# Hybrid-mixer trunk on one core: norm factors applied behind the matmuls instead of in front of them

## What is computed

```
h    = x * rsqrt(mean(x*x) + eps) * norm1_g      # per token factor, per channel weight
proj = h @ w_in                                   # 48 blocks of 128 channels, and dt (16 channels)
gate = sigmoid(h @ w_gate)                        # four branches
x    = x + merged(proj, gate, branches) @ w_out
h2   = x * rsqrt(mean(x*x) + eps) * norm2_g
x    = x + (silu(h2 @ wg) * (h2 @ wu)) @ wd       # layer 0: dense mixer; layer 1: top-2-of-8 experts
```

## Time and profile before

| | us |
|---|---|
| median of 3 runs | 1944.27 |
| lowest, highest | 1943.65, 1946.18 |
| profiled execution, device time | 1946.46 |
| its span, first to last instruction | 1944.6 |
| TensorE busy | 1888.2 (97%) |
| VectorE, ScalarE, GpSimd busy | 1477.2, 1173.1, 313.3 |
| mean granted TensorE clock | 0.993 of full speed |

### The profile page before, as it was taken

How to read it: one execution, slowest core, us unless ns; L and a number is a source line. 1 busy time by engine, 2 the same in 40 slices (tenths; PEclk the granted TensorE clock), 3 DMA queues, 4 the chain that set the end, 5 groups by cost and what they waited for, 6 DMA issues and landing times.

```text
span 1944.6 us, 27985 instructions
## 1 busy us (share of the span) xinstructions
PE 1888.2 (97%) x10637; PEld 1640.5 (84%) x10637; DVE 1477.2 (76%) x1312; ACT 1173.1 (60%) x939; POOL 313.3 (16%) x256
## 2 busy tenths in 40 slices
PE   6999999999999999999999999999999999999997
PEld 6999878899989998778788888888888878888785
DVE  5775667745565775676788988898889888898887
ACT  4555454333335445544677777677776776777775
POOL 1047660000000156920510000000000000000000
PEclk9999999999999999999999999999999999999999
DMA  5444444345543444446599999999999999999994
GB/s 223 174 152 152 173 165 173 138 179 188 178 165 131 174 172 162 146 170 251 199 363 367 359 370 351 361 364 371 360 360 353 381 346 358 374 360 370 355 358 161
DMA packets 71490, 510.80 MB, mean 263 GB/s; under 512 B 7936, under 2 KB 8192, under 8 KB 10368
## 3 DMA queue, kind: packets, MB, share of 16 engines
q1 hardware_dynamic: 70128, 505.15, 69.0%
q0 software_dynamic: 1296, 4.72, 0.6%
HBM read 507.74 MB, written 2.10 MB: 262 GB/s over the span
## 4 chain that ended last, share of the span: by engine, by line
PE 73%; DVE 10%; ACT 6%; POOL 6%; issue 4%; DMA 0%; DVEq 0%; SPq 0%; ACTq 0%; POOLq 0%
PE psum L1270 71%; DVE weight_lo L679 3%; POOL proj_r L1219 3%; POOL proj_r L1220 3%; ACT weight_hi L376 2%; DVE weight_lo L646 2%; DVE scr L792 2%; ACT weight_hi L395 2%; PE psum L1680 1%; ACT y_hi L527 1%; DVE scr L787 1%; ACT proj L447 1%; DVE proj L1013 0%; DMA weight_raw<-mix_w 0%; DVE proj L670 0%
## 5 line engine op out<-in xcount | busy, mean ns | idle before, releaser
L1270 PE MATMUL psum<-weight_hi,y_hi 128*128 128x512 f32 x1440 | 572.3, 397 | 14.1 <-DVE weight_lo L679 11.2
L1270 PE MATMUL psum<-weight_hi,y_lo 128*128 128x512 f32 x1440 | 563.3, 391 | 0.0
L1270 PE MATMUL psum<-weight_lo,y_hi 128*128 128x512 f32 x1440 | 562.5, 391 | 0.0
L646 DVE TENSOR_TENSOR weight_lo<-weight_raw,weight_hi 128x2048 fp32r<-128x2048 f32 x141 | 324.5, 2303 | 236.6 <-ACT weight_hi L376 235.8
L679 DVE TENSOR_TENSOR weight_lo<-weight_raw,weight_hi 128x2048 fp32r<-128x2048 f32 x165 | 377.7, 2289 | 95.7 <-ACT weight_hi L395 95.6
L395 ACT ACTIVATE weight_hi<-proj 128x2048 fp32r<-128x2048 f32 x169 | 324.2, 1925 | 127.5 <-PE psum L1270 127.5
L679 DVE TENSOR_TENSOR weight_lo<-proj,weight_hi 128x2048 fp32r<-128x2048 f32 x169 | 385.6, 2289 | 12.1 <-ACT weight_hi L395 10.6
L1270 PE MATMUL psum<-h_hi,weight_hi 128*128 128x256 f32 x1248 | 359.6, 288 | 9.1 <-DVE h_lo L649 6.4
L1270 PE MATMUL psum<-h_lo,weight_hi 128*128 128x256 f32 x1248 | 356.1, 285 | 0.0
L1270 PE MATMUL psum<-h_hi,weight_lo 128*128 128x256 f32 x1248 | 356.0, 285 | 0.0
L376 ACT ACTIVATE weight_hi<-weight_raw 128x2048 fp32r<-128x2048 f32 x141 | 268.7, 1908 | 142.9 <-PE psum L1270 140.8
(11 more groups left out here) (280 smaller groups left out, 1881.2 us busy)
## 6 DMA issues: line engine op xcount, KB each, us to landing
proj<-moe_w SPq DMA_DIRECT2D x169, 1024.0 KB, 6.2
weight_raw<-moe_w SPq DMA_DIRECT2D x165, 1024.0 KB, 5.9
weight_raw<-mix_w SPq DMA_DIRECT2D x108, 1024.0 KB, 4.8
weight_raw<-ff_w SPq DMA_DIRECT2D x33, 1024.0 KB, 4.7
first_raw<-moe_w SPq DMA_DIRECT2D x2, 1024.0 KB, 5.8
par<-par_in SPq DMA_DIRECT2D x2, 768.0 KB, 9.6
x<-x_in SPq DMA_DIRECT2D x2, 512.0 KB, 4.5
token_rows<-x POOLq DMA_DIRECT2D x2, 512.0 KB, 3.2
```

The lines of the kernel that those rows point to most:

```text
L646: V.tensor_tensor(lo[:, slot, :], raw[:, slot, :], hi[:, slot, :].bitcast(f32), ALU.subtract).then_inc(lo_done, 1)
L1270: return nc.tensor.matmul(o, a, b_, start=start, stop=stop, skip_group_check=True, **k)
```

## The change

The matmuls of the mixers and of the dense mixer run on x times the norm weight, split in high and low, without the factor per token. The factor is applied to the results: VectorE multiplies each bank of the projection by a row of factors (`rstd_row`) as it takes it out of PSUM, where ScalarE copied it before; the gates' sigmoids take it as the scale operand (there tokens lie on the partitions), dt likewise; in the dense mixer VectorE scales both banks, with silu behind the first. The sums and the spread of the factors move on TensorE from in front of unit 0 to the stage dt_row, which stands now behind unit 1, and in the dense mixer to the end and the middle of its first two units. Squares move from VectorE to ScalarE. Convolution 0 moves to behind unit 2. In the dense mixer and into layer 1, x's high and low parts are made behind each output bank. At the start SyncE loads par first, then halves of x and halves of unit 0 by turns, and con behind unit 1. The idle matmuls at the norms go.

```diff
 PLAN = (
-    ("lead", 1), ("dt_row", 1), ("conv0", 1), ("dt_in", 1), ...
+    ("lead", 2), ("dt_row", 1), ("conv0", 0), ("dt_in", 1), ...
 SyncE
-            for half in range(2):
-                sp.dma_start(x[:, 4 * half:4 * half + 4, :], ...)
-            sp.dma_start(con[:], con_in).then_inc(con_loaded, 16)
+            sp.dma_start(par[:, :PAR_FIRST], par_in[0, :, :PAR_FIRST]).then_inc(par_loaded, 16)
+            for part in range(2):
+                sp.dma_start(x[:, 4 * part:4 * part + 4, :], ...)
+                some = slice(part * UNIT // 2, (part + 1) * UNIT // 2)
+                sp.dma_start(raw[:, 0, some], mix_w[0, 0, :, some]).then_inc((first_landed, raw_landed[0])[part], 16)
             for layer in range(DEPTH):
...
-                for j in range(RING):
+                for j in range(0 if layer else 1, RING):
                     load(mix_w[layer, j, :, :], base_of(layer), j)
+                    if layer == 0 and j == 1:
+                        sp.dma_start(con[:], con_in).then_inc(con_loaded, 16)
 ScalarE
+            def high(n, q):
...
+                if n:
+                    act.wait_ge(S["x_sum"], PAIRS * (n - 1) + q + 1)
+                for k in (2 * q, 2 * q + 1):
+                    last = A(to[:, k, :], x[:, k, :], ACT.Copy, scale=gain[:, k:k + 1])
+                last.then_inc(S["h_hi_done"], 1)
+            def squares(q):
+                A(flat(sq[:, 2 * q:2 * q + 2, :]), flat(x[:, 2 * q:2 * q + 2, :]), ACT.Square).then_inc(S["sq_done"], 1)
+            def norm_row(n):
+                act.wait_ge(S["rstd_ps"], n + 1)
+                A(rstd_row[:], bank(7)[:, 0:SEQ], ACT.Copy).then_inc(S["rstd_row"], 1)
             mixer_unit:
                 if u < IN_UNITS:
-                    used(b + u)
-                    A(flat(proj[:, 2 * u:2 * u + 2, :]), bank(u % 4), ACT.Copy).then_inc(S["win_done"], 1)
+                    pass
...
-                        A(gate_of(step)[:, 0, :], bank(0), ACT.Sigmoid).then_inc(S["gate_done"], 1)
+                        A(gate_of(step)[:, 0, :], bank(0), ACT.Sigmoid, scale=rstd[:, 0, :]).then_inc(S["gate_done"], 1)
...
+                elif u >= U_OUT and layer == 0:
+                    high(1, u - U_OUT)
+                    squares(u - U_OUT)
             stage:
                 if kind == "dt_row":
+                    norm_std(2 * layer)
                     act.wait_ge(S["dt_sum"], layer + 1)
                     A(row[:], bank(6)[0:HEADS, 0:SEQ], ACT.Copy).then_inc(S["dt_row"], 1)
+                    norm_row(2 * layer)
             before the units of a layer:
+                if layer == 0:
+                    for part in range(2):
+                        act.wait_ge(x_loaded[part], 16)
+                        high(0, 2 * part)
+                        high(0, 2 * part + 1)
+                        first_half(part)
+                    split(0, 1)
+                    for q in range(PAIRS):
+                        squares(q)
+                else:
+                    for q in range(PAIRS):
+                        high(2 * layer, q)
+                        squares(q)
             dense mixer:
-                        act.wait_ge(unit_used, RING + f0 + 2 + RING * i + 1)
-                        act.wait_ge(S["mult_done"], i + 1)
-                        A(ff_g, bank(4), ACT.Silu).then_inc(S["silu_done"], 1)
+                        act.wait_ge(S["g_scaled"], i + 2)
+                        A(ff_g, ff_g, ACT.Silu).then_inc(S["silu_done"], 1)
 VectorE
+            def low(n, q):
...
+                dve.wait_ge(S["h_hi_done"], PAIRS * n + q + 1)
+                for k in (2 * q, 2 * q + 1):
+                    last = V.scalar_tensor_tensor(to[:, k, :], x[:, k, :], gain[:, k:k + 1], from_hi[:, k, :].bitcast(f32), ALU.mult, ALU.subtract)
+                last.then_inc(S["h_lo_done"], 1)
+            def scaled(out_, b):
+                return V.tensor_tensor(tiles(out_), tiles(bank(b)), rstd_pair, ALU.mult)
+            def evacuated(layer, u):
+                dve.wait_ge(unit_used, RING + base_of(layer) + u + 1)
+                scaled(flat(proj[:, 2 * u:2 * u + 2, :]), u % 4).then_inc(S["win_done"], 1)
             mixer_unit, behind split(b, u + AHEAD):
+                if 2 <= u < IN_UNITS:
+                    evacuated(layer, u)
...
                         dve.wait_ge(unit_used, RING + b + u + 1)
                         added(q)
+                        if q:
+                            low(1, q - 1)
+                        if q == PAIRS - 1:
+                            low(1, q)
             stage:
+                if kind == "dt_row":
+                    norm_diag(2 * layer)
+                    dve.wait_ge(S["rstd_row"], 2 * layer + 1)
+                    evacuated(layer, 0)
+                    evacuated(layer, 1)
                 elif kind == "dt_in":
-                        last = V.tensor_tensor(small[:, 1, t, :], raw_dt[:, t, :], P_("dt_bias"), ALU.add)
+                        last = V.scalar_tensor_tensor(small[:, 1, t, :], raw_dt[:, t, :], rstd[:, t, :], P_("dt_bias"), ALU.mult, ALU.add)
             dense mixer, hidden(i):
-                        V.tensor_tensor(ff_h, ff_g, bank(5), ALU.mult).then_inc(S["mult_done"], 1)
+                        scaled(ff_h, 5).then_inc(S["u_scaled"], 1)
+                        dve.wait_ge(S["u_scaled"], i + 1)
+                        dve.wait_ge(S["silu_done"], i + 1)
+                        V.tensor_tensor(ff_h, ff_g, ff_h, ALU.mult).then_inc(S["mult_done"], 1)
 TensorE
             tile_pair: an argument early; t = 0 and 1 with k < early first, then both with the rest
...
             mixer_unit, u == 0:
+                    elif layer:
+                        tile_pair(0, b, 0, (S["h_lo_done"], 2 * PAIRS * layer), 6)
+                    else:
+                        pe.wait_ge(S["first_lo"], 1)
+                        tile_pair(0, b, 0, (S["h_lo_done"], 0), between=lambda: split_is(0))
             stage:
                 if kind == "dt_row":
+                    pe.wait_ge(con_loaded, 16)
+                    pe.wait_ge(S["masks_done"], 1)
+                    norm_sums(2 * layer)
                     pe.wait_ge(S["wdt_lo"], layer + 1)
...
                     last.then_inc(S["dt_sum"], 1)
+                    norm_spread(2 * layer)
             dense mixer:
-                    tile_pair(4, f0, 0, (S["h_lo_done"], PAIRS))
+                    tile_pair(4, f0, 0, (S["h_lo_done"], PAIRS), 6, a)
+                    norm_sums(1)
                     split_is(f0 + 1)
-                    tile_pair(5, f0, 1)
+                    tile_pair(5, f0, 1, a=a, between=lambda: norm_spread(1))
...
-                        pe.wait_ge(S["silu_done"], i + 1)
+                        pe.wait_ge(S["g_scaled"], i + 1)
```

More of the change, by code:

```diff
@@ L1292, in tile_pair @@
                         last = product(bank(b_out)[:, t * SEQ:(t + 1) * SEQ], (first + j) % RING, KT * t + k,
-                                       h_hi[:, k, :], h_lo[:, k, :], k == 0, k == KT - 1)
+                                       a[0][:, k, :], a[1][:, k, :], k == 0 and (early == KT or t == 0), k == KT - 1)
+                    if n == 0 and between:
+                        between()
                 last.then_inc(unit_used, 1)
```

166 lines of the change are left out of this document (82 added, 84 removed).

## The result

The changed kernel takes **1952.55 us**, the median of 5 runs (1952.28 to 1955.07); the kernel before, timed beside it, 1946.18 (1943.65 to 1946.18, 5 runs). The ratio is 1.0042, with a 95% interval from 1.0029 to 1.0054: slower, by about 0.4%. In the experiments the kernel before was timed 7 to 15 times in each session, and its medians were 1943.4 to 1944.3; against these the difference of the medians is some 8.4 instead of 6.4 (the ratio, made from all runs, says 8.2). The kernel after was timed in the first session alone, five times; where later runs are set against its 1952.55, a difference carries 2 to 3 us of doubt. The profiled execution took 1952.28 us with a span of 1950.5, against 1946.46 and 1944.6 before: +5.9. Forecast were +9.4 and 1953.7.

A forecast was written before the change was run, and what follows sets the result against it. A loop of VectorE and ScalarE, as long as TensorE's work, was taken to become the projection's bound. Start -8.2, dense boundary -2.3, layer 1 -7.6, loop +22.2, clock +5.1, gates +0.2: +9.4 onto 1944.27, 1953.7 us; range 1936 to 1961.

The forecast's parts named there:

- the five places named: Projection: TensorE waits before units 6, 8, the transposes, unit 16 and the spread, released by VectorE; +11.1 us per layer.
- 15 us a layer: Sign that the forecast is right: TensorE's idle time at five places of each projection, released by VectorE.
- The clock, +5.1: TensorE falls to half clock behind new projection waits: three falls more than before, +5.1 us, bounds 0 and 6.8.
- The start, -8.2: Kernel start: first weight matmul at 9.2, unit 2 at 27.2 instead of 35.4, so 8.2 us saved.
- The bound of -4: Kernel start, if halves of weights land later: only 4 of the 8.2 us stay, total 1957.7.
- Into the dense mixer, -2.3: Boundary behind mixer layer 0: a 6.05 us chain per unit, a 4.0 wait, 2.3 us saved; bounds -7.6 and 0.
- The last `down`: End of the dense mixer: one scaling more in front of a wait of 2.06, 0.7 us later.
- Into layer 1: Boundary behind the dense mixer: a wait of 0.8, unit 2 at 590.1 instead of 597.7, so 7.6 us saved.
- the case with GpSimd first: Convolution 6: GpSimd's addition starts before VectorE's pair and holds it up, 1.2 us longer per layer, total 1960.
- Faster: Rival: evacuations hide in VectorE's idle time, boundaries alone count, -18.1 us, total 1926.2; chance 0.18.
- half hidden: Projection: variant of the faster rival, evacuations half hidden, without falls of the clock, total 1937.3.
- Even: Rival: projection loop as worked out, no clock falls in it or the dense boundary, +2.6 us, 1946.9; chance 0.17.

The follow-up runs named there:

- e1: Changed kernel, with ScalarE issuing the split of the next weights ahead of the silu in units of convolutions 1 to 7: 1924.14 us, ratio 0.9898.
- e10: Changed kernel, with VectorE's evacuation of unit u-1 ahead of the low part of unit u+2, in place of unit u's behind it: 1934.56 us, ratio 0.9947.
- e3: Kernel before, with VectorE instead of ScalarE copying the banks of all 24 projection units, as plain copies: 1962.97 us, ratio 1.0100.
- e4: Changed kernel, with ScalarE copying the banks of units 2 to 23 as before, without their token factors: 1934.09 us, ratio 0.9955.
- e11: Kernel before, with idle matmuls in TensorE's waits of over 1.2 us and behind the norm's spread at both boundaries: 1940.88 us, ratio 0.9984.
- e9: Changed kernel, with idle matmuls of ones_r ahead of all long waits of TensorE: 1946.22 us, ratio 1.0016.
- e5: Changed kernel, with ScalarE's high part and squares behind the split of the next output unit in layer 0: 1947.36 us, ratio 1.0011.
- e7: Changed kernel, with 17 idle matmuls in the 4.3 us wait of the first dense unit alone: 1954.5 us.

## Why the prediction was right, and where it was not

**The sign and the mechanism held.** The waits stand at the five places named, and VectorE ends them, before the transposes by way of ScalarE's silu. Forecast were 1.8, 2.2, 2.6, 4.0 and 4.0; the rows have 1.48, 1.92, 0.79 (layer 1: 2.27), 3.93 and 1.98 (layer 1: 0.90). The 0.1 before unit 14 did not show. The sign "15 us a layer" did not come true as it stands: the five waits make 10.1 and 10.5, since a fall of the clock ahead of a wait eats into it. Behind one fall of 1.7 the spread waits 1.98, which makes the 3.7 of the forecast's 4.0. e1 and e10 tell that it is the loop and its order, e3 that the evacuations make 9.4 of the stage's 10.3, e4 that some 1 us per layer is the changed start of the stage. Without falls the stage is 10.3 longer, against 11.2 forecast with the first gate unit: 1.8 too much over both layers.

**The number was in part luck.** The forecast median was 1953.7, the measured one 1952.55. But the forecast difference was +9.4, and +5.9 came between the profiled executions. The boundaries erred by 3.3 one way, loop and clock by 6.9 the other, and the base of the forecast, 1944.27, lay 1.9 below the median of the kernel before that was timed beside the changed one.

**The clock, +5.1, was the worst step.** It counted three more falls in the stages, at full price: four that nothing hides, behind the transposes and the spread of each layer, less the one of before. In the profiled executions it is one (behind the transposes of layer 1) against one (143.9 in layer 0 of before, 142.4 in e11), and net they cost nothing: 8.7 and 11.9 of the table add up to 20.6, which is twice the 10.3 of the runs without falls. What was wrong: falls came also behind the waits of 1.92 and 3.93, where the text had them hidden, and there they were hidden indeed; but by doing so they shortened the next waits, of the transposes (0.79) and of the spread (1.98 and 0.90), and behind these the fall then did not come. In this execution that is in part luck, as one more of the stages could have taken 154.2. Over the whole kernel the changed one has seven stretches against five, and the clock's part is 1.9 to 3.1 by e9 and e11, with the doubt told there.

**The start, -8.2, gave -6.3.** The first weight matmul came at 11.20, not 9.2. The step that failed is ScalarE's: x's first half landed at 5.9, not 5.3; then came a load of ScalarE's function table of 1.28, which was in no term (the kernel before has it too, at 0.71 us, long before its first operation had its input at 7.45; in the changed kernel it began only when x was there); and two high parts take 1.70 (0.85 a pair, not 0.70). Everything behind kept its distance: 9.2 to 27.2 forecast, 11.20 to 29.04 measured. The bound of -4 was not needed, and the halves of the weights were not late.

**Into the dense mixer, -2.3, gave -1.8.** The cycle is 6.2 and the wait 4.31, against 6.05 and 4.0; the high part is again what was mis-sized (0.91 a pair there). That the clock falls behind it was right. e5 shows the chain to be as described.

**The last `down`** waits 2.79, 0.73 more than before, as said. **Into layer 1**, from its end to unit 2, 18.0 us against 17.35: waits of 0.38 and 1.04 in unit 0 where 0.8 was forecast.

So the boundaries gave 3.3 less than forecast (14.8 in place of 18.1), the loop took 1.8 less and the clock's term 5.1 less, which makes +5.8 from +9.4.

**The convolution that meets GpSimd.** Kept at 2.24, measured 2.26 (timeline of VectorE and GpSimd):

```profile
112.61 2.26 DVE L843 TENSOR_SCALAR scr<-proj,par 128x256 f32<-128x256 f32 x2
112.84 1.89 POOL L1252 TENSOR_TENSOR pool_tmp<-proj 128x1020 f32<-128x1020 f32 x1 [86.61 <-DVE proj L715]
```

VectorE's first operation began 0.23 ahead of GpSimd's addition, so the case with GpSimd first did not arise. The pair, 0.61 elsewhere, ended at 114.87, 0.14 behind GpSimd's addition at 114.73, which looks as if its second operation waited for that addition. 0.14 is less than such an operation takes (0.61 for two), so GpSimd's times are rough here, and which of the two held up the other's end is inferred. The rows agree with the rule quoted in the prediction (the Trainium skill, "SBUF — State Buffer", "SBUF: two separate sides").

The price of 1.2 for that case was too high. It was read from the addition's 3.45, but here, begun behind the low part and beside the pair alone, the same addition takes 1.89. In the kernel before it began at 108.80, in the middle of a low part of VectorE that ran from 108.21 to 110.50, and ended 1.75 behind it: the 3.45 hold a wait of 1.7. With GpSimd first the pair would take an estimated 1.89 + 0.61 = 2.50 instead of 2.24, some 0.3 more per layer.

**The rivals.** "Faster", with the evacuations hidden, missed because they stood where VectorE had no idle time; moved by one place (e10) the kernel came out at 1934.6, where "half hidden" had 1937.3. "Even" was the loop without the new falls, 1946.9. e9 takes 1946.22, but the nearness says little: e9 has no falls at all, those of the kernel before included, and against e11, which it answers to, it is 5.3 longer and not 2.6. In the changed kernel the fall at the dense unit came as forecast.

## What to carry to other kernels

When two engines hand work to each other in a fixed order, lay the order out as a loop and compare its length with the time the bottleneck needs for the same units; an engine that is 66% busy (VectorE in the earlier trace rows) can have no room at all where the new work stands. Before giving up a change that lengthens such a loop, look for the hand-over that can be turned round, here a split ahead of a silu that nobody waits for: it was worth 28 us after the change and 10 before it (1952.55 less 1924.14, timed in different sessions, and 1943.37 less 1933.71). A fall of the clock behind a wait costs only if no later wait takes it up, and it can in turn shorten that one; count it last, and for what it leaves.

## What was not expected of the hardware

- Multiplying a bank of 128x512 by a row while copying it out costs VectorE nothing: 686 ns against 684.
- The same addition on GpSimd is listed with 1.89 us or with 3.45, as it began behind VectorE's low part or in the middle of one: a long record can hold a wait.
- Idle matmuls in the waits hold the clock: with them the mean clock went from 0.991 to 0.998 and the kernel after from 1952.55 to 1946.22 us (different sessions), the kernel before from 1944.1 to 1940.88 (the same session), without any change of the other work.
- The same kernel has its falls of the clock in different places from execution to execution, which moves a stage by 1.5 us (152.65, 154.2 and 154.2 for layer 0's stage in the kernel after, e5 and e7, which are the same up to there). Four runs of e7 could not show a gain of one fall.
